# Two 256-column and two 512-column matmuls of a row tile: grouped by width instead of in alternation

## The reference, cut to what matters

```
h = rmsnorm(x) ;  u = h @ w_in                       # 2048 -> 12800 columns
a = silu(layernorm(dwconv31(a_val * sigmoid(a_gate)))) ;  y_a = a @ w_conf_out
y_b = (b_gate * conv3(c_gate * b_h)) @ w_sconv_out
y_c = sliding_window_attention(q, k, v, sinks) @ w_attn_out
x = x + (g0 * y_a + g1 * y_b + g2 * y_c) @ w_mix_out
x = x + square(relu(rmsnorm(x) @ w_up)) @ w_down     # 2048 -> 8192 -> 2048
out = rmsnorm(x)
```

## Time and profile before

| | |
|---|---|
| median of 3 runs | 1580.27 us (1580.24 to 1581.42) |
| span of the profiled execution | 1578.5 us |
| busy share of the span: PE, DVE, ACT | 98%, 71%, 48% |
| chain that ended last | 97% PE |
| DMA | 286.58 MB, mean 182 GB/s |

### The profile page before, as it was taken

The page is one execution under the profiler, slowest core; times in us unless marked ns, Lnnn a source line. Parts: engine busy times, 40 slices in busy tenths (PEclk is TensorE's granted clock), DMA queues, the critical chain, the costliest instruction groups (busy, mean ns, idle before and its releaser), DMA issues.

```text
span 1578.5 us, 25519 instructions
## 1 busy us (share of the span) xinstructions
PE 1550.8 (98%) x8875; PEld 1348.0 (85%) x8875; DVE 1127.0 (71%) x1461; ACT 752.3 (48%) x938; POOL 22.6 (1%) x27
## 2 busy tenths in 40 slices
PE   5999999999999999999999999999999999999997
PEld 5888888888888888888888888888888888888886
DVE  7657888989999988666667665566655665566664
ACT  4444444466664556455445443344434443344443
POOL 5000000000000000000000000000000000000000
PEclk8999999999999999999999999999999999999998
DMA  5665565655445555555555565556555655555552
GB/s 173 193 195 179 178 193 182 205 161 160 159 159 185 188 184 190 186 182 196 182 194 179 184 193 190 180 180 191 192 182 178 193 179 194 187 185 178 195 177 103
DMA packets 285698, 286.58 MB, mean 182 GB/s; under 512 B 9005, under 2 KB 284085, under 8 KB 285652
## 3 DMA queue, kind: packets, MB, share of 16 engines
q1 hardware_dynamic: 285652, 285.98, 56.8%
HBM read 283.32 MB, written 2.10 MB: 181 GB/s over the span
## 4 chain that ended last, share of the span: by engine, by line
PE 97%; DVE 2%; ACT 0%; DMA 0%; issue 0%; ACTq 0%; SPq 0%; DVEq 0%
PE acc L985 59%; PE acc L984 30%; PE acc L981 4%; PE acc L982 2%; DVE h_hl L595 1%; PE acc L989 1%; PE acc L1038 0%; DVE h_hl L591 0%; DVE w_lo L584 0%; DMA x_tok<-in_x 0%; PE acc L1061 0%; PE acc L1060 0%; PE acc L1059 0%; PE acc L994 0%; DVE res L852 0%
## 5 line engine op out<-in xcount | busy, mean ns | idle before, releaser
L985 PE MATMUL acc<-h_hl,w_hi 128*128 128x512 f32 x2460 | 871.6, 398 | 0.0
L580 DVE TENSOR_TENSOR w_lo<-w_raw,w_hi 128x1024 fp32r<-128x1024 f32 x533 | 642.4, 1221 | 237.1 <-ACT w_hi L408 231.7
L408 ACT ACTIVATE w_hi<-w_raw 128x1024 fp32r<-128x1024 f32 x533 | 554.9, 1055 | 451.2 <-PE acc L985 445.5
L984 PE MATMUL acc<-h_hl,w_lo 128*128 128x256 f32 x2460 | 692.2, 281 | 5.8 <-DVE w_lo L584 5.8
L985 PEld LDWEIGHTS acc<-h_hl,w_hi 128*128 128x128 f32 x2460 | 463.8, 189 | 108.4
L984 PEld LDWEIGHTS acc<-h_hl,w_lo 128*128 128x128 f32 x2460 | 466.1, 189 | 11.3 <-issue 5.2
L985 PE MATMUL acc<-m_hl,w_hi 128*128 128x512 f32 x1200 | 424.5, 397 | 0.0
L984 PE MATMUL acc<-m_hl,w_lo 128*128 128x256 f32 x1200 | 337.2, 281 | 0.0
L985 PEld LDWEIGHTS acc<-m_hl,w_hi 128*128 128x128 f32 x1200 | 225.4, 188 | 52.9
L984 PEld LDWEIGHTS acc<-m_hl,w_lo 128*128 128x128 f32 x1200 | 226.6, 189 | 1.7
L510 ACT ACTIVATE second<-acc 128x512 f32<-128x512 f32 x106 | 63.4, 598 | 161.9 <-PE acc L985 161.8
(11 more groups left out here) (156 smaller groups left out, 843.3 us busy)
## 6 DMA issues: line engine op xcount, KB each, us to landing
w_raw<-in_w_in SPq DMA_DIRECT2D x200, 512.0 KB, 3.5
w_raw<-in_w_up SPq DMA_DIRECT2D x128, 512.0 KB, 3.7
w_raw<-in_w_down SPq DMA_DIRECT2D x128, 512.0 KB, 3.3
w_raw<-in_w_mix_out SPq DMA_DIRECT2D x32, 512.0 KB, 4.3
w_raw<-in_w_sconv_out SPq DMA_DIRECT2D x16, 512.0 KB, 3.3
w_raw<-in_w_attn_out SPq DMA_DIRECT2D x16, 512.0 KB, 3.2
w_raw<-in_w_conf_out SPq DMA_DIRECT2D x16, 512.0 KB, 4.1
x_tok<-in_x SPq DMA_DIRECT2D x4, 512.0 KB, 7.6
```

The source lines that it names most:

```text
L408: act.activation(w_hi[:, ahead % RING], w_raw[:, ahead % RING], ACT.Copy).then_inc(hi_done, 1)
L580: dve.tensor_tensor(w_lo[:, q], w_raw[:, q], w_hi[:, q].bitcast(F32), ALU.subtract).then_inc(lo_done, 1)
L984: pe.matmul(*narrow, start=False, stop=False)
L985: last = pe.matmul(*wide, start=False, stop=final)
```

## The change

Within a row tile the four matmuls are issued in another order. Before, for m = 0 and then for m = 1: narrow, wide. After: narrow m = 0, narrow m = 1, wide m = 0, wide m = 1. In the first row tile of a group, where wide comes first: before wide, narrow, wide, narrow; after wide, wide, narrow, narrow. Within each bank the order of accumulation is as before.

```diff
-                    for m in range(2):
-                        w_h, w_l = (w[:, q, a, m * P:(m + 1) * P] for w in (w_hi, w_lo))
-
-                        wide = (acc[:, b + m, :], w_h, act_hl[:, kt, :, :].rearrange("p h n -> p (h n)"))
-                        narrow = (acc[:, b + m, 0:SEQ], w_l, act_hl[:, kt, 0, :])
-                        if first:
-                            pe.matmul(*wide, start=True, stop=False)
-                            last = pe.matmul(*narrow, start=False, stop=False)
-                        else:
-                            pe.matmul(*narrow, start=False, stop=False)
-                            last = pe.matmul(*wide, start=False, stop=final)
+                    wide = [(acc[:, b + m, :], w_hi[:, q, a, m * P:(m + 1) * P],
+                             act_hl[:, kt, :, :].rearrange("p h n -> p (h n)")) for m in range(2)]
+                    narrow = [(acc[:, b + m, 0:SEQ], w_lo[:, q, a, m * P:(m + 1) * P],
+                               act_hl[:, kt, 0, :]) for m in range(2)]
+                    if first:
+                        for m in range(2):
+                            pe.matmul(*wide[m], start=True, stop=False)
+                        for m in range(2):
+                            last = pe.matmul(*narrow[m], start=False, stop=False)
+                    else:
+                        for m in range(2):
+                            pe.matmul(*narrow[m], start=False, stop=False)
+                        for m in range(2):
+                            last = pe.matmul(*wide[m], start=False, stop=final)
                 last.then_inc(slab_used, 1)
```

## The result

The change made the kernel faster by 0.67%: 1570.22 us (median of 4 runs, 1569.20 to 1570.48) against 1580.54 us (4 runs, 1580.24 to 1581.42). The ratio is 0.9933, with a 95% interval of 0.9921 to 0.9945. Run again later beside some of the experiments it gave 0.9935 (0.9920 to 0.9949). The forecast was no visible change, 1581.5 us. The measured time lies outside the forecast's own range (1577 to 1584.5) and inside the wide one (1563 to 1594). It is also near the "half" of rival 1 (1570 us), but by another mechanism, as the experiments show.

The account below looks back on a forecast made before the run. TensorE's own pace was taken as the bound. Unchanged work counted 0 and the new step order +1.3 us, so 1580.27 + 1.3 = 1581.6, stated as 1581.5 us; own range 1577 to 1584.5, 8-in-10 range 1563 to 1594.

Parts of the forecast that it names:

- half: Rival 1 only partly realised: the stream gains half of what the complete fast pace would give, 1570 us.
- rival 1: TensorE's stream settles in the fast pace, 0.347 us a pair: 1561 us if complete, 1570 if half; chance 0.33.
- The bound: Whole span: TensorE, busy 98% at full clock, is the bound; only its start-to-start pace counts, 0.3525 us a pair.
- The moved work: Same matmuls, loads, columns, waits and increments; releases to ACT, DVE and SP at the same distances: cost 0.
- sum of single steps: Per row tile, new wide-wide and narrow-narrow steps, timed at old group seams, add 0.6 ns; 2,144 tiles give +1.3 us.
- What the sum left out: TensorE's pace has a memory; full groups took 0.347 or 0.353 us a pair: bounds -19, +6 or +15 us.
- complete fast pace: All 4,288 pairs on TensorE at 0.347 us: -19 us, 1561 us.
- Rival 2: Second narrow to first wide matmul: weight loads under narrow matmuls come late; 7 ns a tile, +15 us, 1595 us; chance 0.30.
- 325 ns a pair: TensorE's pair by the skill page, columns plus 2.5 ns each: no order could matter, change exactly 0; measured pair longer.
- Rival 3: TensorE's stream shortens, but waits for the weights' low half eat the gain: 1578 us; chance 0.02.

Follow-up runs that it names:

- strict alternation: Against the kernel before: every row tile wide 0, narrow 0, wide 1, narrow 1, so no width repeats at group boundaries; 1582.15 us (0.9995), run again 1574.93 us (0.9960).
- its form without seams: Against the change: all row tiles, the first too, wide 0, wide 1, narrow 0, narrow 1; 1568.55 us (0.9921 to the kernel before), repeated 1568.37 us.
- four and four: Against the kernel before: blocks of two row tiles, four wide matmuls then four narrow; 1577.65 us, ratio 0.9978.
- eight and eight: Against the kernel before: a whole slab (four row tiles) at a time, eight wide matmuls then eight narrow; 1571.09 us, ratio 0.9941.

## Why the prediction was wrong, point by point

**The bound** was read rightly. TensorE's pace is nearly all that moved; ACT, DVE and SP followed, and the start and the tail stayed within about half a us.

**The moved work** was costed at nothing, and was nothing: releases, waits and counts are unchanged.

**The step that failed** is the sum of single steps, "+1.3 us, since these are the very steps and 134 and 145 of them agree with the old ones". In the kernel after, over all starts, wide to wide takes 0.2329 us (2,258 steps), wide to narrow 0.2331, narrow to narrow 0.1157 (2,253 steps), narrow to wide 0.1162. Every kind of step is shorter, by 0.7 to 2.0 ns, the two old kinds too. A row tile so takes 697.9 ns instead of 703.0 (2 x 0.2346 + 2 x 0.1169 us), and 2,144 x 5.1 = 10.9 us is the gain, against 11.1 between the spans. The distance isn't a property of who follows whom, it belongs to the beat in which the whole stream runs. The steps at the seams were measured inside the old beats.

**What the sum left out** was named with its size: the two paces of full groups in the earlier trace rows, and that a new order might settle in the better, the worse, or a third. It was the third. The experiments show that strict alternation has two beats (0.3467 and 0.3533 us a pair). Two and two has one (0.3483), which all four profiles of the change and of its form without seams showed wherever nothing stands between the slabs, the first slab of a group in the change apart. The kernel before has the slow one for most of its span. Its run times keep together, while without seams they fall into two heaps. Against the slow beat two and two gains 5 ns a pair, against the fast one it loses 1.6.

**Rival 1** had the right sign and a wrong end: the new order didn't settle in the fast pace (0.3467 us a pair) but in the one of its own, 0.3483, all through. That its "half", 1570 us, is the measured time is luck. No run reached the complete fast pace; its -19 us stay an estimate, and the fastest run of strict alternation, 1567.23 us, is 13 below the kernel before.

**Rival 2** had the loads of narrow matmuls in a row come late. For the change it is refuted at the very place that it named: the distance from the second narrow matmul to the first wide one is 0.1162 us in the kernel after, where narrow to wide took 0.1169 before. With narrow matmuls alone the step settles at 120 ns and doesn't grow. Blocks of four and eight have longer narrow steps than the change, on average up to these 120 ns and not above. By the rule of the Trainium skill (TensorE: Matmul & The Clock Gate, LDWEIGHTS), a load takes its columns over 1.2 GHz, by estimate 107 ns, as long as the columns of a narrow matmul. No run shows that as a cost: the step of 120 ns is 13 above either. The page's formula that was weighed in the prediction (TensorE: Matmul & The Clock Gate, Back-to-back issue gap, 2.5 ns beyond the columns) is called there that of an isolated matmul; for a stream in which each matmul has its load, the Trainium skill says that both set the spacing. So the prediction's 325 ns a pair was not what the page gives for such a stream. The formula gives by estimate 109 and 216 ns for the two widths, where one width alone took 120 and 227 here, with five times as much beyond the columns. That no order could matter, which the prediction concluded from it, is wrong for this stream.

**Rival 3** doesn't show: the waits for the low half didn't grow.

Open stays what makes the beats: why strict alternation can hold two, why four and four is slower than both two and two and eight and eight, and, without seams, what at the beginning of a stretch picks the beat. That the 13.3 ns belong to the weight load was not tried.

## What to carry to other kernels

Where TensorE is busy throughout, compare the time per matmul between stretches that have the same instructions: if it differs at the same clock, the stream has more than one beat, and the order of widths is worth a few runs. A step that is seen at a seam tells little of what a stream of such steps will cost; the mean of single steps can't be added up when the pace has a memory. Measure the pace with one width throughout (here 13.3 ns above the columns). No order tried here held a pace below the sum of the two, so that the sum gives an estimate of what another order may still bring: here 0.3483 - 0.3467 us a pair, 4,288 x 0.0016 = 7 us.

## What the runs showed of the hardware

Matmuls of 512 and 256 columns, alternating in float32, run in one of two stable beats, 1.9% apart, at the same granted clock and with the same succession of matmuls. Without seams one repeats every two pairs, the other every three. A single row tile in another order is enough to throw the stream from one into the other. The same kernel, strict alternation without seams, gave 1567 to 1570 us in seven runs and 1580 to 1583 in sixteen. Its median is the outcome of chance, and three runs of it could have shown either. Repeating each width twice gave a single beat, and 17 runs of the two such kernels that were run twice, the change and its seamless form, stayed within 1567.1 to 1571.3 us.
